# Sums of squares of the RMS norms as four products side by side, in a one-core two-block transformer kernel

## The reference, cut to what matters

```python
def rmsnorm(x, g):
    xf = x.astype(jnp.float32)
    y = xf * lax.rsqrt(jnp.mean(xf * xf, axis=-1, keepdims=True) + EPS)
    return (y * g.astype(jnp.float32)).astype(x.dtype)
...
    for i in range(DEPTH):          # 2 layers; layer 0 a conv module, layer 1 attention
        hx = rmsnorm(x, norm_g[i, 0]) * (1.0 + sc_x) + sh_x
        ...                         # yx = conv or attention module of hx
        x = x + g_x * rmsnorm(yx, norm_g[i, 1])
        fx = rmsnorm(x, norm_g[i, 2]) * (1.0 + scf_x) + shf_x
        x = x + gf_x * rmsnorm(swiglu(fx, ...), norm_g[i, 3])
```

## Time and profile before

| what | value |
|---|---|
| median of 3 runs | 2318.43 us (2317.78 to 2322.64) |
| profiled execution | 2318.18 us, span 2316.4 us |
| TensorE, products | 2108.1 us busy, 91% of the span |
| DVE / ACT / POOL | 1220.9 / 996.7 / 427.1 us busy |
| mean granted TensorE clock | 0.93 of 2.4 GHz |
| `sums`, L537 (all users) | 336 weight loads, 59.9 us; 336 products, 61.7 us |
| `spread`, L552 (all users) | 108 products, 22.5 us |

### The profile page before, as it was taken

How to read it: one execution, slowest core, us unless ns; L and a number is a source line. 1 busy time by engine, 2 the same in 40 slices (tenths; PEclk the granted TensorE clock), 3 DMA queues, 4 the chain that set the end, 5 groups by cost and what they waited for, 6 DMA issues and landing times. The chain is left out here.

```text
span 2316.4 us, 33850 instructions
## 1 busy us (share of the span) xinstructions
PE 2108.1 (91%) x13724; PEld 1848.3 (80%) x13724; DVE 1220.9 (53%) x2441; ACT 996.7 (43%) x1814; POOL 427.1 (18%) x230
## 2 busy tenths in 40 slices
PE   6997688999999799889999888999998888898998
PEld 3853566888886576779998777989998778898997
DVE  4788325323333455455566554567456745467464
ACT  4321434222232335544444445446454445445554
POOL 0000010000001113500000111253552111143524
PEclk8998678999997798989999999999999989999999
DMA  8331424222222134255554432545554343354551
GB/s 327 100 137 45 145 79 138 94 95 97 97 94 73 57 126 164 74 190 181 183 166 128 136 111 92 157 144 173 183 183 139 98 145 102 110 173 145 189 178 62
DMA packets 84537, 307.33 MB, mean 133 GB/s; under 512 B 9376, under 2 KB 10656, under 8 KB 84000
## 3 DMA queue, kind: packets, MB, share of 16 engines
q1 hardware_dynamic: 84384, 305.19, 39.3%
HBM read 304.10 MB, written 1.05 MB: 132 GB/s over the span
## 5 line engine op out<-in xcount | busy, mean ns | idle before, releaser
L461 PE MATMUL pb<-Hh,whi 128*128 128x256 f32 (+1 forms) x2832 | 890.1, 314 | 70.3 <-DVE MOD L1721 18.7
L462 PE MATMUL pb<-Hl,whi 128*128 128x256 f32 (+1 forms) x2832 | 878.1, 310 | 0.0
L463 PE MATMUL pb<-Hh,wlo 128*128 128x256 f32 (+1 forms) x2832 | 877.8, 310 | 0.0
L1690 DVE TENSOR_TENSOR wlo<-raw,whi 128x1024 fp32r<-128x1024 f32 x325 | 408.0, 1259 | 446.0 <-ACT whi L1061 444.9
L461 PEld LDWEIGHTS pb<-Hh,whi 128*128 128x128 f32 x2832 | 557.6, 197 | 100.9 <-issue 45.7
L1061 ACT ACTIVATE whi<-raw 128x1024 fp32r<-128x1024 f32 x468 | 489.5, 1053 | 328.7 <-PE pb L463 315.5
L462 PEld LDWEIGHTS pb<-Hl,whi 128*128 128x128 f32 x2832 | 557.7, 197 | 22.9
L463 PEld LDWEIGHTS pb<-Hh,wlo 128*128 128x128 f32 x2832 | 556.7, 197 | 23.0
L2474 POOL TENSOR_TENSOR wlo<-raw,whi 128x1024 fp32r<-128x1024 f32 x143 | 343.5, 2415 | 925.9 <-ACT whi L1061 925.8
L2482 POOL TENSOR_TENSOR X<-X,tmpb 128x512 f32<-128x512 f32 (+1 forms) x12 | 16.6, 1382 | 744.8 <-DVE tmpb L1784 744.8
L1830 DVE SCALAR_TENSOR_TENSOR Y<-U,VEC,Y 128x512 f32<-128x512 f32 x180 | 120.5, 743 | 0.0
(11 more groups left out here) (273 smaller groups left out, 2685.5 us busy)
## 6 DMA issues: line engine op xcount, KB each, us to landing
raw<-wstream SPq DMA_DIRECT2D x572, 512.0 KB, 3.4
X<-xin SPq DMA_DIRECT2D x2, 1024.0 KB, 9.4
CON<-consts SPq DMA_DIRECT2D x1, 1182.0 KB, 8.4
out<-X SPq DMA_DIRECT2D x8, 128.0 KB, 1.7
VEC<-vecs SPq DMA_DIRECT2D x1, 662.0 KB, 9.7
CON<-consts SPq DMA_DIRECT2D x1, 130.0 KB, 6.4
VEC<-vecs SPq DMA_DIRECT2D x1, 88.0 KB, 2.0
```

What stands on the lines that cost most here:

```text
L461: e.matmul(dst, hi, xh, start=k == 0, stop=False)
L462: e.matmul(dst, hi, xl, start=False, stop=False)
L463: i = e.matmul(dst, lo, xh, start=False, stop=k == kt - 1)
L1690: e.tensor_tensor(wlo[:, i, :], raw[:, p % NRAW, :], f32(whi[:, i, :]), ALU.subtract).then_inc(sig("dve_lo", ("lo", p)), 1)
```

## The change

The roles in the product are swapped: 32 columns of `mean` (1/1024) are the stationary operand, and the squares are the moving one, in four quarters of n/4 columns, each into its own 32 partitions of PSUM (`quarters`). The sums of the tokens then lie in [128, n/4], each value repeated on the 32 partitions of its group. Square root and reciprocal work on that tile (`root4`, `rec4`), in a scratch tile of the ring `s`. `widen` takes the place of `spread`: the stationary operand is a column of the new constant `quad` (1/32 on one group of 32 partitions, zero elsewhere) broadcast to 128x128, the moving one the tile of n/4 columns; always four products. In the norms of the first kind DVE adds only squares 1 to 6; square 7 stays in its own buffer and gets a set of quarters of its own, in the same accumulation. The conv layer norm, the head norms and the second block keep `sums` and `spread`.

```diff
+            def quarters(S, tile, n, start, stop, point):
+                b = slots.at(("stat", S))
+                for c in range(4):
+                    i = e.matmul(b[32 * c:32 * c + 32, 0:n // 4], con("mean", 0, 32), tile[:, c * n // 4:(c + 1) * n // 4],
+                                 start=start, stop=stop)
+                i.then_inc(sig("pe_stat", point), 1)
+
             def acc_sums(S, n):
-                b = bank("pst", ("stat", S), ("root", S))
+                bank("pst", ("stat", S), ("root", S))
                 w.wait_ge(*con_in)
                 w.wait_ge(*on("acc", S))
-                sums(S, slots.at(("acc", S)), b, n, True, True, ("sums", S))
+                quarters(S, slots.at(("acc", S)), n, True, False, ("asum", S))
+                w.wait_ge(*on("sq", S, 7))
+                quarters(S, slots.at(("sq", S, 7)), n, False, True, ("sums", S))
+
+            def widen(S, n, *until):
+                b = bank("pt", ("spread", S), *until)
+                r = slots.at(("root", S))[:, 0:n // 4]
+                w.wait_ge(*on("rec", S))
+                for c in range(4):
+                    i = e.matmul(b[:, c * n // 4:(c + 1) * n // 4], con("quad", c, c + 1).broadcast_to((128, 128)), r,
+                                 start=True, stop=True)
+                i.then_inc(sig("pe_stat", ("spread", S)), 1)
...
-                    sums(R, slots.at(("sq", R, k)), b, n, k == 0, k == 7, ("sums", R) if k == 7 else ("xsum", R, k))
+                    quarters(R, slots.at(("sq", R, k)), n, k == 0, k == 7, ("sums", R) if k == 7 else ("xsum", R, k))
...
-            spread("r0", 512, [("mt", "n1", 7)])
+            widen("r0", 512, ("mt", "n1", 7))
...
+            def root4(S, n):
+                t = buf(1 if n == 512 else 4, "s", ("root", S), ("spread", S))
+                w.wait_ge(*con_in)
+                w.wait_ge(*on("sums", S))
+                e.activation(t[:, 0:n // 4], slots.at(("stat", S))[:, 0:n // 4], ACT.Sqrt, bias=con("eps6")).then_inc(
+                    sig("act_root", ("root", S)), 1)
...
-                points = [("accadd", S, k)] + ([("acc", S)] if k == 7 else [])
+                points = [("accadd", S, k)] + ([("acc", S)] if k == 6 else [])
...
+            def rec4(S, n):
+                t = slots.at(("root", S))[:, 0:n // 4]
                 w.wait_ge(*on("root", S))
                 e.reciprocal(t, t).then_inc(sig("dve_rec", ("rec", S)), 1)
...
-            acc_add("y0", 7, 512)
...
+    put("quad", (i[:, None] // 32 == np.arange(4)[None, :]) / 32.0)
```

More of the change, by code:

```diff
@@ L138, in vec_plan @@
     return off, at
-CONSTS = (("eps6", 1), ("eps5", 1), ("pick", 2), ("ident", 128), ("mean", 128), ("ones", 128), ("mean4", 128), ("mean128", 128),
+CONSTS = (("eps6", 1), ("eps5", 1), ("pick", 2), ("quad", 4), ("ident", 128), ("mean", 128), ("ones", 128), ("mean4", 128), ("mean128", 128),
           ("mean64", 128), ("rot1", 128), ("rot2", 128), ("dup0", 128), ("dup1", 128), ("cos1", 256), ("sin1", 256),
@@ L556, in residual @@
             def residual(R, S, n):
-                spread(S, n, [("rdone", R, 7)])
+                widen(S, n, ("rdone", R, 7))
             def x_sums(R, n, every=2):
-                b = bank("pst", ("stat", R), ("root", R))
+                bank("pst", ("stat", R), ("root", R))
                 for k in range(8):
                     w.wait_ge(*on("sq", R, k))
-                    sums(R, slots.at(("sq", R, k)), b, n, k == 0, k == 7, ("sums", R) if k == 7 else ("xsum", R, k))
+                    quarters(R, slots.at(("sq", R, k)), n, k == 0, k == 7, ("sums", R) if k == 7 else ("xsum", R, k))
                     if k % every == 0:
@@ L575, in tensor @@
             bite(2)
-            spread("x0", 512, [("mt", "n0", 7)])
+            widen("x0", 512, ("mt", "n0", 7))
             mod_tr(1)
@@ L648, in tensor @@
             mod_tr()
-            spread("r1", 512, [("mt", "n2", 7)])
+            widen("r1", 512, ("mt", "n2", 7))
             def head_sums(key, n):
@@ L768, in tensor @@
             x_sums("r2", T, 4)
-            spread("r2", T, [("mt", "n3", 7)])
+            widen("r2", T, ("mt", "n3", 7))
             bite(99)
@@ L1089, in acc_square @@
                 else:
-                    t = buf(stage, "sq", ("sq", S, k), ("accadd", S, k))
+                    t = buf(stage, "sq", ("sq", S, k), ("accadd", S, k) if k < 7 else ("sums", S))
                 e.activation(shape(t), src, ACT.Square).then_inc(sig("act_sq", ("sq", S, k)), 1)
@@ L1119, in scalar @@
             row(1, "S", 1)
-            root("x0", 4, ("spread", "x0"))
+            root4("x0", 512)
             preload(ACT.Sigmoid)
@@ L1205, in residual @@
             def residual(R, S, n, name, after):
-                root(S, n // 128, ("spread", S))
+                root4(S, n)
                 for k in range(8):
@@ L1212, in residual @@
                         row(1 if n == 512 else 4, name, 1)
-                root(R, n // 128, ("spread", R))
+                root4(R, n)
             residual("r0", "y0", 512, "F", 0)
@@ L1367, in scalar @@
             hi_to(("down", 1, 1, 7), 5)
-            root("y3", 2, ("spread", "y3"))
+            root4("y3", T)
             for k in range(8):
@@ L1713, in rec @@
                 t = slots.at(("root", S))[:, 0:cols]
+                w.wait_ge(*on("root", S))
+                e.reciprocal(t, t).then_inc(sig("dve_rec", ("rec", S)), 1)
+            def rec4(S, n):
+                t = slots.at(("root", S))[:, 0:n // 4]
                 w.wait_ge(*on("root", S))
@@ L1766, in residual @@
                 r = slots.at(("spread", S))
-                rec(S, n // 128)
+                rec4(S, n)
                 w.wait_ge(*on("ma", l, slot))
@@ L1796, in residual @@
                 if pool:
-                    rec(R, n // 128)
+                    rec4(R, n)
                 else:
@@ L1801, in residual @@
                     low(7)
-            for k in range(1, 8):
+            for k in range(1, 7):
                 acc_add("x0", k, 512)
-            rec("x0", 4)
+            rec4("x0", 512)
             for g in range(4):
@@ L1926, in ffn @@
                         lo_to(("down", l, pi, 7), 5)
-                acc_add(Yk, 7, n)
             ffn(0, FFN0, 512, "y1", MOD_F[1:])
@@ L2053, in vector @@
                     acc_add("y2", m - 1, T)
-            acc_add("y2", 7, T)
             residual("r2", "y2", 1, 1, 1)
```

## The result

| kernel | median | runs |
|---|---|---|
| before | 2318.65 us | 2317.78 to 2322.64, 4 runs |
| changed | 2288.1 us | 2286.23 to 2289.8, 4 runs |

The profiled execution took 2287.43 (span 2285.7).

The account below looks back on a forecast made before the run. TensorE was taken as the bound, with the sums of r0 to r2 at its low clock. Terms -7.2 - 8.6 - 2.0 - 1.7 - 0.1 - 0.1 + 0.7 = -19.0 from 2318.18 gave 2299 us, range 2290 to 2306.

Parts of the forecast that it names:

- A set: In r0 and r1 a set of quarters takes 0.65 us alone, 0.55 in a row, against 1.76 before.
- (c): Rival, chance 0.06: quarters stream one after the other, loads hidden; a set stays at 1.76 us; 2321 us.
- (d): Rival, chance 0.05: each pass also waits for its own load; a set is 2.2 us; +13, 2332 us.
- r0, step by step: Norm r0 followed up to widen, starting at 334.15 where the spread started at 341.38: -7.2 us.
- r1: Norm r1, in the same order as r0: 8.4 us saved to the last sum, 0.2 more for set 0: -8.6.
- r2: Norm r2, on half the columns: -2.0 us taken, between -1.4 at the low clock and -3.7 at the high.
- rival (a): Chance 0.22: the clock comes back around the second bite; r0 saves 3.0, r1 3.4, r2 1.5 more; 2291 us.
- the gaps at squares 3 and 6: TensorE's waits for these squares in r0 remain; held against the clock coming back, no size given.
- The reciprocal: In the norms, 1.07 us for 128 columns, 0.61 for 64, at 7.2 ns a column; +0.9 and +0.45.
- The first kind: Norms x0 and y0 to y3: x0 0, y0 -0.1, y1 -1.7, y2 -0.1, y3 +0.7; -1.2 us in all.
- r1's cover: In r1, mod_tr (3.55 us) ahead on TensorE hides root and reciprocal; without it -7.2 us, not -8.6.
- Rival (b): Chance 0.10: the clock is lower for longer, also in linears behind r0 and r1; 5 to 7 us back; 2305.

Follow-up runs that it names:

- e3: The changed kernel with norms x0 and y0 to y3 back in the old form, only r0 to r2 new; 2291.08 us, ratio 0.9882.
- e4: The changed kernel with norms r0 to r2 back in the old form, only x0 and y0 to y3 new; 2320.13 us, ratio 1.0005.
- e8: The changed kernel with all bites of r0 to r2's sums moved behind widen, r1's mod_tr too; 2309.89 us, ratio 0.9959.
- e10: The changed kernel unaltered, measured again; 2290.2 us, ratio 0.9865.
- e1: The kernel before, with 128 identical moving columns in place of one in the sums of r0 to r2; 2298.09 us, ratio 0.9906.
- e7: The changed kernel with the reciprocal of the eight norms replaced by a copy of the same size; 2285.64 us, ratio 0.9856.
- e2: The changed kernel with the four quarters of a set one after the other, each with a full 128x128 stationary; 2312.18 us, ratio 0.9963.

## Why the prediction was wrong, point by point

- **What bounds the kernel**: right. The sets of r0 to r2 were the bound, e3 and e4 show it, and 30.2 of the 30.7 us come out of these three stretches. (The 19.8 us of eight sets and three bites are 0.5 more than the stretch that they were set equal to, 321.55 to 340.8, because set 0 took only 1.31 there; the forecast does not hang on it.)
- **A set**: right for the level it was worked out at, 0.65 alone (0.66, and 0.65 in e8) and 0.55 in a row. Rivals (c) and (d), 1.76 and 2.2 a set, are out; by its own terms (d) should have come to 2331, not 2332.
- **The failed step is the clock in "r0, step by step", r1 and r2**: it took bites at 1.9, the later sets at 0.55 to 0.65, `widen` at 2.08, `mod_tr` at 3.55, all of 1.2 GHz. In r0 the level rose at 326, during the second bite. Up to set 3, before the rise, forecast and trace agree: 4.45 and 4.32 us behind the end of the first square. From there they part. In r0 the first square to `widen` took 10.3 us, not 13.2 (before 20.5), and behind it, `widen` to the first `modulated`, 4.4 in place of 6.65, which I had left as it was. In r1 the level was high until about 722, at 0.50 for some 6 us, and back before `mod_tr`, which took 1.95 for 3.55. In r2 the level stayed high all the way in the first trace, -4.4 for my -2.0; in e10 it did not, and r2 is -2.2, so that my -2.0 is right for one execution and wrong for the other. The misses of the three stretches are 5.3, 4.7 and 2.4, together 12.4; the whole was off by 11.6, since the rest of the kernel gave 0.4 where I had 1.2. I had this as rival (a), with its mechanism and its place (around the second bite), gave it 0.22, and priced it at -8: about two thirds of what it was.
- **Why I gave it so little**: I took the gaps at squares 3 and 6 for evidence against. The row that I should have weighed was there: in the earlier trace rows TensorE was never idle and the level was still low, so it wasn't idleness that kept it there. What the sets made TensorE do, one moving column behind each full load, was. e1 shows that directly.
- **The reciprocal**: 0.95 and 0.55 us for 1.07 and 0.61. The slope from 8 columns to 128 is (953 - 203)/120 = 6.3 ns a column, a little less than the 7.2 between 2 and 8, so carrying on from rows of the same operation was right where the other DVE row (0.28) would have been too low by a factor of over three.
- **The first kind**: -1.2 forecast, nothing measured in the whole (e4 1.0005). For y0 the working held: table, root, reciprocal, and the spread comes 0.3 us earlier, for the -0.1 forecast. y1 came out at -1.9 up to `widen`, for -1.7, but by luck: the working kept the low level, and 1.2 of the 1.9 came with the high one.
- **r1's cover**: right. `mod_tr` (729.75 to 731.7) hides root and reciprocal, and e7 gets nothing back in r1.
- **Rival (b)**, 5 to 7 us given back by slower linears behind r0 and r1: not seen behind r0 (FFN 0 is 2.3 shorter). Behind r1 attention is 2.3 and 2.0 longer in the two traces of the changed kernel, but that stretch varies by more than this, so nothing is shown either way.
- **x0**: right, TensorE still waits 1.48 for the transfer behind the sums, 0.49 before:

```profile
24.82 1.07 PE L507 MATMUL pb<-raw,csz 128*32 128x512 f32 x8 [1.48 <-DMA raw<-wstream]
```

## What to carry to other kernels

Before costing a faster step at the clock that it has now, ask whether the step itself keeps the clock there: a TensorE that is busy all the time at the low level is the sign, and then the work around the step (here bites, spread, `mod_tr`) can get faster with it. Sum over partitions with the data as the moving operand, not as the weights, and put four such products side by side where the result allows it; the reciprocal on the wider result costs its columns, so lay it where another engine's work covers it. Filler work between short steps is not only hidden there: in r0 of this kernel the clock came back only with it and the quarters together, and it kept the weight stream moving (e8).

## What the runs showed of the hardware that was not expected

- TensorE busy without a gap from 323 to 340.8 in r0 of the kernel before, three bites and otherwise sums with one moving column per load of 128x128, was granted 0.50 all the time (the earlier trace rows is a part of it). In e1, just as busy, with 128 moving columns in the sums, it was granted 0.50 until 326 and 1.00 from there on, and in e2's r1 1.00. In e2's r2, with 64, it was 0.50, in one trace. The Trainium skill, "TensorE: Matmul & The Clock Gate" (What's actually happening), has the throttle follow how busy the array has been; these rows show that a busy row of the profile is not yet that.
- Products of 32 stationary columns overlap across different steps too. In the changed kernel the bite starts at 321.51, while the set ahead of it runs until 321.77, and the weights of the bite are loaded from 321.30. (The profile models the ends of products; the same overlap behind a full set is 0.08 in the kernel before, 324.80 + 5.28 against 330.00.)

```profile
321.08 0.23 PEld L545 LDWEIGHTS pb<-tmpb,CON 128*32 128x32 f32 x8 [3.44 <-issue]
...
321.30 0.44 PEld L507 LDWEIGHTS pb<-raw,csz 128*32 128x32 f32 x8
```

- The DVE reciprocal is far slower per column than a copy: 953 ns for 128 columns and 553 for 64, and 230 for a copy of the same 128 columns (e7):

```profile
L1746 DVE RECIPROCAL tmpb<-tmpb 128x128 f32<-128x128 f32 x5 | 4.8, 953 | 17.0 <-ACT tmpb L1109 17.0
L1746 DVE RECIPROCAL tmpb<-tmpb 128x64 f32<-128x64 f32 x3 | 1.7, 553 | 6.4 <-ACT tmpb L1109 6.4
```
